# Output projections with 512 moving columns, interleaved norms of expert outputs, reloads issued by SyncE

## What is computed

```python
# first block, each layer l
y = jnp.einsum('bsc,cd->bsd', mixed * jax.nn.silu(gate), w_out[l])
h_res = _layer_norm(DEEPNORM_ALPHA * h_res + y, ln_g[l], ln_b[l])

# second block, each layer l (the context's rows likewise in layer 0)
o = jnp.concatenate([o_a, o_b, o_c], axis=-1) @ w_out[l]
x = layer_norm(DEEPNORM_ALPHA_2 * x + g1 * o, ln1_g[l], ln1_b[l])
h2 = modulate(x, sh2, sc2)
x = layer_norm(DEEPNORM_ALPHA_2 * x + g2 * ec_moe(h2, w_router[l], w_gate[l], w_up[l], w_down[l]),
               ln2_g[l], ln2_b[l])
# the next layer begins with: h = modulate(x, sh1, sc1) = layer_norm(x) * (1 + scale) + shift

# ec_moe: for each of 16 experts, its 64 best tokens (32 of the context):
hid = jax.nn.silu(xs @ w_gate) * (xs @ w_up)      # 1024 x 1024 weights each
y[idx] += (hid @ w_down) * gate
```

## Time and profile before

| | |
|---|---|
| median of 3 runs | 2948.76 us |
| all runs | 2946.39, 2948.76, 2959.36 us |
| profiled execution | 2945.61 us, its span 2943.5 us |
| granted TensorE clock, mean | 0.952 |
| busy: PE, DVE, ACT, POOL | 2575.9, 1002.3, 731.5, 242.3 us |
| DMA | 577.92 MB, mean 196 GB/s |

### The profile page before, as it was taken

The page is one execution under the profiler, slowest core; times in us unless marked ns, Lnnn a source line. Parts: engine busy times, 40 slices in busy tenths (PEclk is TensorE's granted clock), DMA queues, the critical chain, the costliest instruction groups (busy, mean ns, idle before and its releaser), DMA issues. The chain is left out here.

```text
span 2943.5 us, 46207 instructions
## 1 busy us (share of the span) xinstructions
PE 2575.9 (88%) x18738; PEld 1511.9 (51%) x18738; DVE 1002.3 (34%) x2212; ACT 731.5 (25%) x1889; POOL 242.3 (8%) x290
## 2 busy tenths in 40 slices
PE   7999999999999889896999999938889969777873
PEld 3564694665686566596444444416566843222220
DVE  3022440213345664556111222146643541111112
ACT  2234311333321344422112111122433221000100
POOL 1000100000101000011000100011100111000101
PEclk9999999999999999997999999978999979999997
DMA  7342615344612002016799999961102169999995
GB/s 222 90 132 80 177 36 143 106 125 107 168 50 73 1 19 60 30 58 248 272 400 401 402 392 400 380 173 36 28 1 79 68 249 404 399 404 404 404 404 232
DMA packets 299209, 577.92 MB, mean 196 GB/s; under 512 B 12512, under 2 KB 236096, under 8 KB 249920
## 3 DMA queue, kind: packets, MB, share of 16 engines
q1 hardware_dynamic: 283744, 523.44, 49.3%
q0 software_dynamic: 15184, 52.42, 6.2%
q10 hardware_dynamic: 144, 0.14, 0.0%
HBM read 552.84 MB, written 23.10 MB: 196 GB/s over the span
## 5 line engine op out<-in xcount | busy, mean ns | idle before, releaser
L447 PE MATMUL ps<-turned,ring 128*128 128x512 f32 (+1 forms) x1408 | 551.4, 552 | 10.2 <-ACT turned L1430 8.8
L1082 PE MATMUL ps<-ring,turned 128*32 128x512 f32 (+1 forms) x2208 | 378.5, 607 | 47.3 <-DMA ring<-in_w_gate 45.2
L447 PEld LDWEIGHTS ps<-turned,ring 128*128 128x128 f32 x1408 | 270.8, 194 | 279.8 <-issue 259.0
L1243 DVE SCALAR_TENSOR_TENSOR turned<-turned,gates,work 64x1024 f32<-64x1024 f32 (+1 forms) x48 | 61.3, 1276 | 505.6 <-ACT turned L1182 280.8
L693 PE MATMUL ps<-ring,mixT 128*128 128x128 f32 x2048 | 232.5, 276 | 0.8 <-DVE mixT L1565 0.8
L693 PEld LDWEIGHTS ps<-ring,mixT 128*128 128x128 f32 x2048 | 231.0, 193 | 1.3 <-DVE mixT L1565 1.3
L1082 PEld LDWEIGHTS ps<-ring,turned 128*32 128x32 f32 (+1 forms) x2208 | 92.0, 120 | 190.2 <-DMA ring<-in_w_gate 81.4
L493 PE MATMUL ps<-kz,qz 96*128 96x256 f32 (+3 forms) x384 | 163.1, 512 | 24.0 <-DVE qz L1982 8.7
L1159 ACT ACTIVATE work<-ps 128x512 f32<-128x512 f32 x32 | 19.1, 597 | 573.0 <-PE ps L1082 292.7
L1593 ACT ACTIVATE probs_v<-ps,col 128x256 f32<-128x256 f32 (+5 forms) x216 | 136.5, 632 | 70.6 <-DVE col L1543 34.9
L1606 ACT ACTIVATE probsT<-ps 128x512 f32<-128x512 f32 (+3 forms) x280 | 120.3, 456 | 133.4 <-PE ps L533 106.2
(11 more groups left out here) (273 smaller groups left out, 3178.0 us busy)
## 6 DMA issues: line engine op xcount, KB each, us to landing
ring<-in_w_gate SPq DMA_DIRECT2D x120, 1024.0 KB, 13.2
ring<-in_w_up SPq DMA_DIRECT2D x64, 1024.0 KB, 14.4
mixT<-in_w_up SPq DMA_DIRECT2D x64, 1024.0 KB, 14.4
ring<-in_w_mod SPq DMA_DIRECT2D x96, 512.0 KB, 3.9
ring<-in_w_in SPq DMA_DIRECT2D x82, 512.0 KB, 7.2
mixcT<-in_w_down SPq DMA_DIRECT2D x32, 1024.0 KB, 13.1
probs_v<-in_w_down SPq DMA_DIRECT2D x32, 1024.0 KB
qz<-in_w_down SPq DMA_DIRECT2D x32, 1024.0 KB
```

The source lines that it names most:

```text
L447: mm = nc.tensor.matmul(ps[:, b, 0:n], w[:, k, :], rhs[:, k, 0:n], start=(k == 0), stop=(k == KD - 1))
L1082: mm = nc.tensor.matmul(ps[o:o + step, dst, :], lhs[:, k, g:g + step], w[:, half * 512:(half + 1) * 512], start=(k == 0), stop=(k == KD - ...
L1243: ins = nc.vector.scalar_tensor_tensor(ye[R, :], ye[R, :], g, grow[R, r, :], ALU.mult, ALU.mult)
```

## The change

Five things are changed together.

1. `w_out` is loaded by rows: slot k holds rows 128k to 128k + 127 with all 1024 columns. `pe_out` makes each half one sum over eight k with 512 moving columns. The last use of all eight slots is then the last tile's half 1.
2. `dve_norm` is split into `dve_norm_stats`, `dve_norm_centre` and `dve_norm_scale`. In `dve_moe_out` the next tile's statistics and centring stand in front of the present tile's last scaling.
3. `act_moe_out` issues the root of the head and the root of the next tile's norm ahead of the head's evacuation.
4. SP instead of POOL waits for the last scatter and issues the reloads; between the layers they stand in its queue after the first twelve weight loads of layer 1.
5. SP instead of POOL issues the final stores and waits for them.

```diff
+        def w_rows(w, l, k):
+            return w[l, k * P:(k + 1) * P, :].rearrange("p (k n) -> p k n", k=KD)
...
             for half in range(2):
                 job = ("out", st, t, half)
-                ws = [slot(pe, s) for s in slots[4 * half:4 * half + 4]] if first else [
-                    ring[:, banks.get(("slot", s), (0, 16))[0], :].rearrange("p (k n) -> p k n", k=KD)
-                    for s in slots[4 * half:4 * half + 4]]
                 b = open_job(pe, job)
                 tl = t - NT if ctile(t) else t
-                for c in range(4):
-                    for k in range(KD):
-                        mm = nc.tensor.matmul(ps[:, b, c * P:(c + 1) * P], lhs[:, k, tl * P:(tl + 1) * P],
-                                              ws[c][:, k, :], start=(k == 0), stop=(k == KD - 1))
+                for k in range(KD):
+                    if first and half == 0:
+                        slot(pe, slots[k])
+                    w = ring[:, banks.get(("slot", slots[k]), (0, 16))[0], half * 512:(half + 1) * 512]
+                    mm = nc.tensor.matmul(ps[:, b, :], lhs[:, k, tl * P:(tl + 1) * P], w, start=(k == 0),
+                                          stop=(k == KD - 1))
                 mm.then_inc(*done("job_done", job))
-                if last:
-                    for s in slots[4 * half:4 * half + 4]:
+                if last and half == 1:
+                    for s in slots:
                         last_use(s, job)
...
-            out += [(w1(l, "wo", c), w_cols(a["w_out"], l, c * P)) for c in range(8)]
+            out += [(w1(l, "wo", k), w_rows(a["w_out"], l, k)) for k in range(KD)]
...
         def dve_moe_out(dve, l):
...
+            def begin(t):
                 dve.wait_ge(sem(f"y_landed{t}"), 16 * (l + 1))
                 if t == 0:
                     dve.wait_ge(sem("rows_landed"), rows_landed(st))
-                last = l == DEPTH - 1
-                dve_norm(dve, (st, t), res(t), res(t), rows_of(st),
-                         final=("out_ready", t) if last else ("dve_step", ("b", (st, t))))
+                dve_norm_stats(dve, (st, t), res(t))
+                dve_norm_centre(dve, (st, t), res(t), res(t), rows_of(st))
...
+            begin(tiles[0])
+            for n, t in enumerate(tiles):
+                if last and n + 1 < len(tiles):
+                    begin(tiles[n + 1])
+                end(t)
                 if not last:
-                    dve.wait_ge(*at("dve_step", ("b", (st, t))))
-                    dve_head(dve, ("pre", l + 1), t)
+                    head_begin(t)
+                    if n + 1 < len(tiles):
+                        begin(tiles[n + 1])
+                    head_end(t)

         def act_moe_out(act, l):
...
+            act_root(act, (st, tiles[0]), LN_EPS_2)
+            for n, t in enumerate(tiles):
+                if not last:
+                    act_root(act, (nx, t), LN_EPS_2)
+                if n + 1 < len(tiles):
+                    act_root(act, (st, tiles[n + 1]), LN_EPS_2)
+                if not last and not ctile(t):
+                    act_head(act, nx, t, root=False)
...
-                pool.wait_ge(*nth("scattered", l, EXPERTS - 1, 16))
-                for t in tiles:
-                    pool.dma_start(res(t), a["y_moe"][l][t * P:(t + 1) * P, :]).then_inc(sem(f"y_landed{t}"), 16)
-            for t in range(NT):
-                pool.wait_ge(*at("out_ready", t))
-                pool.dma_start(a["out"][t * P:(t + 1) * P, :], h[:, t, :]).then_inc(sem("out_stored"), 16)
-            pool.wait_ge(sem("out_stored"), 16 * NT)
...
+            def moe_reload(l):
+                sp_.wait_ge(*nth("scattered", l, EXPERTS - 1, 16))
+                for t in range(NT + NC if l == 0 else NT):
+                    sp_.dma_start(res(t), a["y_moe"][l][t * P:(t + 1) * P, :]).then_inc(sem(f"y_landed{t}"), 16)
+
             for l in range(DEPTH):
-                for item in second_block_slots(l):
+                for n, item in enumerate(second_block_slots(l)):
+                    if l > 0 and n == RING:
+                        moe_reload(l - 1)
                     load_slot(sp_, *item)
...
+            moe_reload(DEPTH - 1)
+            for t in range(NT):
+                sp_.wait_ge(*at("out_ready", t))
+                sp_.dma_start(a["out"][t * P:(t + 1) * P, :], h[:, t, :]).then_inc(sem("out_stored"), 16)
+            sp_.wait_ge(sem("out_stored"), 16 * NT)
```

More of the change, by code:

```diff
@@ L1495, in dve_moe_out @@
         def dve_moe_out(dve, l):
-            st = ("experts", l)
+            st, nx = ("experts", l), ("pre", l + 1)
             tiles = list(range(NT + NC)) if l == 0 else list(range(NT))
-            for t in tiles:
+            last = l == DEPTH - 1
+            def begin(t):
                 dve.wait_ge(sem(f"y_landed{t}"), 16 * (l + 1))
```

57 lines of the change are left out of this document (36 added, 21 removed).

## The result

| | before | after |
|---|---|---|
| median of 5 runs each | 2952.84 us | 2933.55 us |
| all runs | 2946.39, 2948.76, 2952.84, 2956.73, 2959.36 | 2929.09, 2931.33, 2933.55, 2935.36, 2937.03 |
| ratio, 95% interval | | 0.9940 [0.9927, 0.9953] |
| profiled execution, its span | 2945.61, 2943.5 us | 2931.33, 2929.2 us |
| granted clock, mean | 0.952 | 0.951 |

The kernel is 0.6% faster. The forecast said 2923.5 us; in the profiled executions 14.3 us are gained where it had 24.1.

A forecast was written before the change was run, and what follows sets the result against it. PE paced the output projections, DMA the expert stages, a chain of single steps the layer boundary and end. 10.1 + 5.4 + 0.6 + 0.3 + 7.7 = 24.1 us off 2945.61 gave 2921.5, plus 2: 2923.5 us, range 2915 to 2934.

The forecast's parts named there:

- term 3: Two reloads issued by SP instead of POOL: 0.3 us saved each, 0.6 in all, bounds -0.5 and 2.
- 1 output projections: 18 tile projections with 512-column products: 13.73 instead of 14.29 us a tile, 10.1 us saved on PE's path.
- 2 between the layers, norms: First norm to last latent head's scaling: 27.6 instead of 33.0 us, 5.4 us saved, bounds 4.0 and 6.0.
- term 4: Last norms and stores at the end: norms 0.5 us shorter, some 0.2 lost to store spacing, 0.3 us saved.
- DVE never waits: Between the layers, the new order leaves DVE only its own work, 27.6 us up to the fourth head's scaling.
- first bytes within 1 us of the issue: Sign for the reloads: the first reload's bytes come within 1 us of SP issuing it.
- The third rival: Small packets ahead of the reload: 1.6 us lost, up to 3 with a late eighth weight tile; 2925 to 2928; chance 0.07.
- The drain: At the end, POOL's 7542 ns drain finishes before the last store, SP's short one remains: 7.7 us saved, bounds 0 and 8.
- the drain stays: Rival at the program's end: SP or POOL pays the 7.5 us again after the last store; 2931.2 us, chance 0.20.
- The expert streams swallow it: Rival: expert stages' start does not move with PE, so mixer projections and boundary gain nothing; 2934.5 us, chance 0.08.
- Slower: Rival in both transfer-bound stages: 392 GB/s throughout makes them 3% longer, 30 us; 2954 us, chance 0.03.
- the likeliest case: The forecast itself for the whole kernel: 2923.5 us, own range 2917 to 2930, chance 0.62.

The follow-up runs named there:

- the last experiment: Changed kernel with modulation rows behind the reload, DVE also scaling the fourth latent head before beginning the first context tile: 2919.88 us, ratio 0.9895.
- modulation rows later: Changed kernel, but modulation rows wait for the sixth reloaded tile while the router's weights go right behind the scatter: 2925.23 us, ratio 0.9909.

## Why the prediction was right in four terms and wrong in one

Direction and four of five terms held, and the term that failed is number 3. In the profiled executions the gain is 9.8 us short of the forecast: 6.0 of that are term 3 and 4.1 lie where the code is the same; the other terms brought 0.3 more than forecast. In medians the gain is 4.8 us short, 19.3 against 24.1. The rest of the 10 us by which the time missed is the step from the profiled execution to the median, for which the prediction added 2 us: the median of the kernel before, over five runs, lies 7.2 us above its profiled execution, and over 53 further ones some 4 us.

| term | forecast | in the whole (profile) | alone (medians) |
|---|---|---|---|
| 1 output projections | 10.1 | 9.6 | 9.5 |
| 2 between the layers, norms | 5.4 | 5.65 | 5.5, with term 4's norms |
| 3 reloads from SP | **0.6** | **-5.4** (-6.1 and +0.7) | **-4.1** |
| 4 and 5 last norms, stores, drain | 8.0 | 8.5 | 8.0 for the stores |
| elsewhere, same code | 0 | -4.1 | |
| sum | 24.1 | 14.3 | |

1. **Output projections: right.** 13.73 us a tile, as worked out from L447's 429.1 ns. The four stages went from 274.71 to 265.07 us. Of the 0.5 us missing 0.4 are in the first stage, which lost 1.84 instead of 2.24; the granted clock in its first 4 us was 0.57, against 0.65 before. Per instruction removed it is 0.56 us / 96 = 5.8 ns (the 5.9 is a slip). What these are, the runs leave open: with a quarter of the instructions the weight loads are a quarter too, and PEld's busy time in a tile falls from 14.29 to 6.03 us.
   The Trainium skill, "TensorE: Matmul & The Clock Gate", "Wait — 56ns, not 53.3ns?", gives about 2.5 ns a warm matmul, and the prediction counted it once per instruction of the trace: 4.3 us. The four stages, 9.0 us shorter with the projections alone, stand against that count. They do not stand against the page: it measures 55.6 ns for a warm matmul of 128 columns, and an fp32 instruction of 128 columns takes 111.6 ns here, twice that. With two such costs in each instruction the page gives an estimate of 96 x 5 ns x 18 = 8.6 us. No run shows how an fp32 instruction is made up.
2. **Between the layers: right in size.** From first statistics to the fourth head's scaling 1954.56 to 1981.93, 27.4 us, against a forecast of 27.6. The step as put, "DVE never waits", is off by one wait: the first tile's scaling waits 0.46 us for its own centring. The context tile counted as a cost of the new order, 2.76 us, turned out to be cover for 1.86 us of waiting: only the last experiment shows that.
3. **Reloads from SP: the term that failed.** The issue by SP itself brings about what was forecast: SP's reload reaches DVE 3.25 us (modulation rows later) and 3.13 us (at the end) after its issue, POOL's took 3.60 and 3.66; 0.35 and 0.5 us gained. What failed is the step "POOL now sends them while the scatter is still in flight, and the reload cannot start before that has landed, so most lies beside the scatter. I take 0, and 1.6 as the other end". The order of events was right, the conclusion was not. The pieces do not lie beside the scatter at no cost: from its issue to SP's reload it takes 7.7 us, without them 5.4. And their effect does not end when it has landed: the reload reaches DVE 7.5 us after its issue instead of 3.25, and the sign that the prediction named, first bytes within 1 us of the issue, did not come (full rate after 6 us). The price of 1.6 us, the other end of the range, came from one row of 1 us at 83% and 27 GB/s; the share of a single microsecond is no measure for such pieces, as the 1.63 above shows, and it was no count of pieces times a duration. The third rival had the place of the loss, at a chance of 0.07 and at 1.6 us (the rest of its range was a late eighth weight tile); its price was 6.1. That the pieces cause the loss is shown; in what way they hold up the scatter, SP's issue and the reload is not.
4. **Last norms: right.** 2910.16 to 2926.08, 15.9 us, as forecast.
5. **The drain: right.** It begins at 2902.1, with POOL's last issue (2902.35), and lies beside the norms. The rival "the drain stays" is refuted by the changed kernel and by the run with the stores alone, and the run in which POOL stores one tile brings it back. The Trainium skill, "VectorE: DVE Perf Modes", "The DRAIN you can't avoid", gives some 12 ns, on every engine, for the drains that the runtime puts ahead of and behind a kernel. The closing ones here stand at a line of the kernel itself, L139, and fit the figure only in part: SP's take 7 to 123 ns, DVE's 1324 to 2301, POOL's 6440 to 11608.

**The sum.** The remaining 4.1 us of the profiled execution are 2.35 in the first block's layer 1, 2.72 in mixer 1, 0.61 before the first projection, less 0.74 and 0.77 elsewhere and rounding. The first is shown above to vary by 12 us with the same code. For mixer 1 the changed kernel has a granted clock of 0.93 over 315.58 us and the kernel before 0.94 over 312.86; the stretch took 312.20 to 315.58 us in the kernels with the new order and 312.49 to 315.41 in those without, so it is likely the same thing, but no run isolates it. In medians, with the pieces out of the way, the kernels took 2925.23 and 2925.53 us, 24.4 and 24.3 us below the kernel before, where the forecast had 24.1. With four runs each their intervals reach from 22 to 32 and from 20 to 31 us; that the agreement is so close is luck.

**The other rivals.** "The expert streams swallow it" is refuted: projection end to last scatter took 589.28 and 589.23 us, so the whole shift was passed on. "Slower" by a stream at 392 GB/s did not occur: 542.17 us became 541.40 from the last projection's end to the last scatter. The range of 2915 to 2934 us reached the time only at its upper end; the likeliest case's own, 2917 to 2930, did not.

## What to carry to other kernels

When a wait leaves an engine's queue, list every transfer behind it and where it lands now; do not price small ones by their bytes: 16 KB in 2048 pieces of 8 B cost 6 us in front of a critical reload and nothing that shows behind it. POOL's stream ended with a drain of 6 to 12 us in every kernel here: let another engine issue and await the last DMA. And before work is moved off a path, look at what wait it covers.

## What the runs showed of the hardware that was not expected

- Pieces of 8 B, written from SBUF to DRAM between a scatter and a reload, delayed the reload's arrival by 3.7 ns each between 1024 and 2048 of them and by 4.8 between 2048 and 4096. 1024 pieces of 64 B, read, and 256 of 64 B, written, cost nothing in the same place.
- They slow down other queues as well: from a scatter's issue to the reload's, which waits for its landing, 5.4 us became 6.5 to 7.7, with no order by their number; the first tile of SP's reload came after 7.5 to 8.1 us instead of 3.3 with 2048 pieces and after 18.0 with 4096; and SP's own issue of four loads took 4.15 to 4.79 and 13.93 us instead of 1.76.
- POOL's closing drain: 7542 ns in the three kernels where POOL reloads and stores, 6685 where it only stores, 6440 behind one store, 11608 behind four reloads, and 8967 to 9157 in the eight where its stream ends with the scatter. SP's took 7 ns where it had waited for stores, else 122 or 123.
